# Moving projection work between the query/key tiles, and modulation products into the attention and the merge, in a two-block transformer kernel

## The reference

```python
mod_x = silu(c) @ ada_w + ada_b                      # 6*1024 columns
sh1, sc1, g1, sh2, sc2, g2 = split(mod_x, 6)
hx = modulate(rmsnorm(x, norm1_g), sh1, sc1)         # h * (1 + sc) + sh
px = hx @ w_in                                       # 512 + 256 + 128 + 32 + 2048 columns
fx, qlx, kvlx, krx, gx = split_proj(px)              # Fourier input, latents, gates
kx, vx = mla_kv(kvlx, krx, ...)                      # also for the 256 context rows
qx = mla_q(qlx, ...)                                 # 8 heads of 96, RMS norm and rotation
att_x = latent_attention(qx, keys of x and ctx, values)
g = sigmoid(gx + b_gate)                             # gf | ga, 1024 each
y = gf * (fourier_mix(fx) @ w_fourier) + ga * (att_x @ w_mla_o)
x = x + g1 * (y @ w_out)
x = x + g2 * sq_relu_mlp(modulate(rmsnorm(x, norm2_g), sh2, sc2), w_up, w_down)
```

## Time and profile before

| what | value |
|---|---|
| median of 3 runs | 2515.11 us (2514.92 to 2517.38) |
| the profiled execution: time, span | 2515.88 us, 2514.1 us |
| PE, PEld busy | 93%, 75% of the span |
| DVE, ACT, POOL busy | 40%, 32%, 33% |
| mean granted clock of PE | 0.965 |
| query/key tiles, first sum to first score | 118.13 to 209.55 us |
| attention, first score to last value | 209.55 to 332.6 us |
| Fourier input, then DFT begins | 336.13 to 358.00 us |
| first `wfa` product, last `out1` product | 393.95 and 547.5 us |

### The profile page before, as it was taken

How to read it: one execution, slowest core, us unless ns; L and a number is a source line. 1 busy time by engine, 2 the same in 40 slices (tenths; PEclk the granted TensorE clock), 3 DMA queues, 4 the chain that set the end, 5 groups by cost and what they waited for, 6 DMA issues and landing times.

```text
span 2514.1 us, 29045 instructions
## 1 busy us (share of the span) xinstructions
PE 2329.7 (93%) x11804; PEld 1874.0 (75%) x11804; DVE 998.1 (40%) x1609; ACT 811.5 (32%) x1184; POOL 818.3 (33%) x234
## 2 busy tenths in 40 slices
PE   7758999989999979989898999999899899999998
PEld 3535788867888868878787788667588788788887
DVE  3685623142111246564636320533536345322202
ACT  3333532223222325242424222333423343222212
POOL 0746323433344423020211133122133332344342
PEclk9877999989999989999999999999999899999999
DMA  6412122222332222010101023112123231223321
GB/s 233 134 50 84 51 78 84 93 92 67 101 100 89 95 88 75 26 51 18 51 18 51 17 84 109 51 43 88 46 77 108 79 123 64 81 90 100 100 98 53
DMA packets 178610, 197.47 MB, mean 79 GB/s; under 512 B 3412, under 2 KB 170816, under 8 KB 178496
## 3 DMA queue, kind: packets, MB, share of 16 engines
q1 hardware_dynamic: 176848, 190.84, 23.6%
q10 hardware_dynamic: 1648, 5.02, 0.5%
HBM read 193.76 MB, written 2.10 MB: 78 GB/s over the span
## 4 chain that ended last, share of the span: by engine, by line
PE 81%; DVE 6%; issue 2%; ACT 2%; POOL 1%; DMA 0%; ACTq 0%; DVEq 0%; POOLq 0%
PE ps L1824 20%; PE ps L1826 19%; PE ps L1825 19%; PE ps L2120 3%; PE ps L1924 3%; PE ps L2086 2%; PE ps L2324 1%; PE ps L2315 1%; PE ps L2082 1%; PE ps L2322 1%; POOL w_lo L599 1%; PE ps L1918 1%; PE ps L1871 1%; PE ps L1873 1%; PE ps L1872 1%
## 5 line engine op out<-in xcount | busy, mean ns | idle before, releaser
L599 POOL TENSOR_TENSOR w_lo<-raw,w_hi 128x2048 fp32r<-128x2048 f32 (+1 forms) x150 | 681.1, 4541 | 1485.9 <-ACT w_hi L673 1485.9
L1824 PE MATMUL ps<-h_hi,w_hi 128*128 128x512 f32 x1384 | 561.4, 406 | 21.6 <-POOL w_lo L599 6.0
L1826 PE MATMUL ps<-h_hi,w_lo 128*128 128x512 f32 x1384 | 544.9, 394 | 0.0
L1825 PE MATMUL ps<-h_lo,w_hi 128*128 128x512 f32 x1384 | 544.1, 393 | 0.0
L673 ACT ACTIVATE w_hi<-raw 128x2048 fp32r<-128x2048 f32 x150 | 285.6, 1904 | 395.7 <-PE ps L1826 394.6
L1824 PEld LDWEIGHTS ps<-h_hi,w_hi 128*128 128x128 f32 x1384 | 263.3, 190 | 101.5 <-issue 39.2
L1826 PEld LDWEIGHTS ps<-h_hi,w_lo 128*128 128x128 f32 x1384 | 262.7, 190 | 57.4
L1825 PEld LDWEIGHTS ps<-h_lo,w_hi 128*128 128x128 f32 x1384 | 263.7, 191 | 50.1
L1824 PE MATMUL ps<-g_hi,w_hi 128*128 128x512 f32 x256 | 100.9, 394 | 0.0
L1826 PE MATMUL ps<-g_hi,w_lo 128*128 128x512 f32 x256 | 100.4, 392 | 0.0
L1825 PE MATMUL ps<-g_lo,w_hi 128*128 128x512 f32 x256 | 99.4, 388 | 0.0
(11 more groups left out here) (370 smaller groups left out, 4052.1 us busy)
## 6 DMA issues: line engine op xcount, KB each, us to landing
raw<-w_in SPq DMA_DIRECT2D x48, 1024.0 KB, 5.2
raw<-w_down SPq DMA_DIRECT2D x27, 1024.0 KB, 5.1
raw<-ada_w SPq DMA_DIRECT2D x24, 1024.0 KB, 5.2
raw<-w_gate_up SPq DMA_DIRECT2D x22, 1024.0 KB, 5.1
raw<-w_up SPq DMA_DIRECT2D x16, 1024.0 KB, 5.5
raw<-w_mkv SPq DMA_DIRECT2D x8, 1024.0 KB, 5.6
raw<-w_out SPq DMA_DIRECT2D x4, 1024.0 KB, 5.2
raw<-w_a_out SPq DMA_DIRECT2D x4, 1024.0 KB, 5.2
```

The costliest lines, as they stand in the source:

```text
L599: nc.gpsimd.tensor_tensor(w_lo[:, split_at[u] % 2, 0:n], raw[:, u % 2, 0:n], w_hi[:, split_at[u] % 2, 0:n].bitcast(F32), ALU.subtract).the ...
L1824: T.matmul(out_, wh, hi, start=start, stop=False, skip_group_check=True)
L1825: T.matmul(out_, wh, lo, start=False, stop=False, skip_group_check=True)
L1826: return T.matmul(out_, wl, hi, start=False, stop=stop, skip_group_check=True)
```

## The change

What it does, part by part:

- **Unit order.** `f0` stands before `lat_kv`, `f1` and the four `gf` units behind it; then 12 instead of 16 modulation blocks; the last four stand between the units of the merge.
- **Tiles.** PE does `f0` before `lat_kv`, `f1` in pieces around the latent statistics, and in each of the tiles m = 0 to 7 four pieces of a `gf` unit (`FILL`). ACT stores `gf` as sigmoid at m = 1, 3, 5, 7. The tile's own banks move from 0 and 1 to 2 and 3 for odd m.
- **Residual.** The sigmoid of `gf` is kept in `xT`. `xT` itself is written to DRAM before (2 MB, issued by ACT) and read back in 8 parts during the merge.
- **Modulation.** Eight of the 16 later blocks stay on POOL, which begins them only after the tenth `qk_mm`. Eight go to DVE, with eight chained instructions of 256 columns each: blocks 2, 5, 8 and 11 behind items 11, 17, 23 and 29 of the attention, blocks 12 to 15 at the end of the merge steps j = 0 to 3. The matmuls of `modulation` stand at item 27, behind the attention, and in the MLP.
- **Fourier part.** The DFT begins right behind the attention, with pieces of `ga0` and `ga1` between its steps.

```diff
+    wide("f0", "f", t["w_in"], 0, 0)
     wide("lat_kv", "kv", t["w_in"], 0, FOUR_W + Q_LORA, 4)
-    for j in range(8, 24):
+    wide("f1", "f", t["w_in"], 0, 256)
+    for j in range(4):
+        wide("gf", "gf", t["w_in"], 0, GATE1_COL + 256 * j)
+    for j in range(8, 20):
         wide("ada_b", "ada", t["ada_w"], 0, 256 * j, 0, False)
-    for j in range(2):
-        wide("f", "f", t["w_in"], 0, 256 * j)
-    for j in range(4):
-        wide("merge1", "gf", t["w_in"], 0, GATE1_COL + 256 * j)
-        wide("merge1", "ga", t["w_in"], 0, GATE1_COL + D + 256 * j)
+    MERGE1 = [("ga", 0), ("ga", 1), ("wfa", 0), ("ada", 12), ("ga", 2), ("wfa", 1), ("ada", 13), ("ga", 3), ("wfa", 2),
+              ("ada", 14), ("wfa", 3), ("ada", 15)]
...
+    BY_VECTOR = [2, 5, 8, 11, 12, 13, 14, 15]
+    BY_POOL = [a for a in range(16) if a not in BY_VECTOR]
+    BATCH = [range(0, 8), range(8, 12), range(12, 16)]
+
+    def ada_row_of(a):
+
+        if 8 <= a < 12:
+            return tmp2[:, :, :].rearrange("p a (b c) -> p (a b) c", c=256)[:, a - 8, :]
+        return ada_sum[:, a % 8, :]
...
+    ADA_TURN, ADA_ITEM, ADA_BANK = {11: 2, 17: 5, 23: 8, 29: 11}, 27, [6, 6, 5]
...
+        return 4 if m % 2 == 0 else 2
+
+    FILL = [4] * 8 + [0, 0]
...
+                elif ada_units.index(u - 2) - 8 in BY_POOL:
+                    sp.wait_ge(sem["ada_by_pool"], BY_POOL.index(ada_units.index(u - 2) - 8) + 1)
                 else:
-                    sp.wait_ge(sem["ada_summed"], ada_units.index(u - 2) - 7)
+                    sp.wait_ge(sem["ada_by_vector"], BY_VECTOR.index(ada_units.index(u - 2) - 8) + 1)
...
-            for u in range(first["merge1"]):
+            for u in range(first["merge1"] + 2):
                 load(u)
             sp.wait_ge(sem["at_out"], 32)
             sp.dma_start(dft[:, :], t["dft"]).then_inc(sem["dft_in"], 16)
-            load_phase("merge1")
+            for u in range(first["merge1"] + 2, last_of["merge1"]):
+                load(u)
...
+                if a == 0:
+                    pool.wait_ge(sem["c_silu"], 2)
+                    pool.wait_ge(sem["qk_mm"], 10)
...
+            act.dma_start(x_kept, xT[:, :, :].rearrange("p k c -> p (k c)")).then_inc(sem["x_out"], 16)
...
+                if m in fill_done:
+                    j = fill_done[m]
+                    for jj in range(2):
+                        store_tile(first["gf"] + j, jj, xT[:, 2 * j + jj, :], ACT.Sigmoid, bias=col("b_gate", 2 * j + jj))
+                    if j < 2:
+                        next_hi()
...
-            attention("one", prob1, probT1, QK1 ** -0.5, at_hi, (20, 25))
-
-
-            for j in range(2):
-                for jj in range(2):
-                    store_tile(first["f"] + j, jj, f_T[:, 2 * j + jj, :])
-                next_hi()
+            attention("one", prob1, probT1, QK1 ** -0.5, at_hi, (30, 31))
...
+                        act.dma_start(xT[:, k, :], x_kept[:, k * S:(k + 1) * S]).then_inc(sem["x_back"], 16)
...
+            def modulate(a):
+
+                u, dst = ada_units[8 + a], ada_row_of(a)
+                dve.wait_ge(w_in_slot[u % 2], load_count[u])
+                dve.wait_ge(sem["c_silu"], 2)
+                link(V.tensor_scalar(dst, raw[:, u % 2, 0:256], silu_c[:, 0, 0:1], None, ALU.mult))
+                for k in range(1, KT):
+                    ins = V.scalar_tensor_tensor(dst, raw[:, u % 2, k * 256:(k + 1) * 256], silu_c[:, k, 0:1], dst,
+                                                 ALU.mult, ALU.add)
+                    if k < KT - 1:
+                        link(ins)
+                ins.then_inc(sem["ada_by_vector"], 1)
...
+                    if kind == "one" and n in ADA_TURN:
+                        modulate(ADA_TURN[n])
+                    if kind == "one" and n == ADA_ITEM:
+                        modulation(0)
...
+                modulate(12 + j)
...
+            wide_gemm(first["f0"], h_hi, h_lo)
...
+            for k in range(3, 6):
+                piece(first["f1"], k)
             qk_mm(0)
             qk_mm(1)
+            for k in range(6, KT):
+                piece(first["f1"], k)
+            filled = 0
             for m in range(10):
                 if m < 8:
                     qk_mm(m + 2)
+                for i in range(FILL[m]):
+                    piece(first["gf"] + filled // KT, filled % KT)
+                    filled += 1
                 qk_turn(m)
...
-                wide_gemm(first["f"] + j, h_hi, h_lo)
...
+            for i in range(2):
+                u = merged("ga", i)
+                over_channels(2 * i)
+                over_channels(2 * i + 1)
+                for k in range(5):
+                    piece(u, k)
+                over_tokens(2 * i)
+                over_tokens(2 * i + 1)
+                for k in range(5, KT):
+                    piece(u, k)
+            pe.wait_ge(sem["fm_lo_done"], 4)
...
```

More of the change, by code:

```diff
@@ L414, in tile_count @@
         return val([x + j + 1 for x in tile_at], u, loop)
+    tile_bank, tile_turn = [], []
+    per_bank, n_rot = [0] * 4, 0
+    for u, x in enumerate(units):
+        banks = []
+        for j in range(x.tiles):
+            if first["f1"] <= u < first["ada_b"]:
+                banks.append(j)
+            else:
+                banks.append(n_rot % 4)
+                n_rot += 1
+        tile_bank.append(banks)
+        for b in banks:
+            per_bank[b] += 1
+        tile_turn.append([per_bank[b] for b in banks])
     def bank_of(u, j):
-        return (tile_at[u] + j) % 4
+        return tile_bank[u][j]
     def bank(u, j):
@@ L423, in stored_count, with merged @@
     def stored_count(u, j, loop=None):
-        return val([(x + j) // 4 + 1 for x in tile_at], u, loop)
+        return val([x[j] if j < len(x) else 0 for x in tile_turn], u, loop)
+    def merged(kind, j):
+        return first["merge1"] + MERGE1.index((kind, j))
     def slot_before(u):
@@ L490, in qk_bank @@
     def qk_bank(m):
-        return 4 if m % 2 == 0 else 0
+        return 4 if m % 2 == 0 else 2
+    FILL = [4] * 8 + [0, 0]
+    fill_done, _n = {}, 0
+    for _m, _k in enumerate(FILL):
+        for _i in range(_k):
+            _n += 1
+            if _n % KT == 0:
+                fill_done[_m] = _n // KT - 1
     qk_sq = sq2[:, :, :].rearrange("p a c -> p (a c)")[:, 0:H1 * QK1]
@@ L625, in _ @@
                 if u == first["ada_b"]:
-                    for a in range(16):
+                    for a in BY_POOL:
                         modulate(a)
-                    u += 16
+                    u += 12
                     continue
@@ L766, in _ @@
                 store_tile(u, j, lat_q[:, j, :])
+            next_hi()
+            for j in range(2):
+                store_tile(first["f0"], j, f_T[:, j, :])
+            next_hi()
             store_tile(v, 0, lat_kv[:, 0:S])
@@ L817, in _ @@
             v_and_square(0)
+            for j in range(2):
+                store_tile(first["f1"], j, f_T[:, 2 + j, :])
+            next_hi()
+            act.wait_ge(sem["x_out"], 16)
             for m in range(10):
@@ L1532, in mlp_chunk @@
                                         ALU.subtract).then_inc(sem["g_lo_done"], 1)
+                if isinstance(count0, int) and count0 == 0:
+                    modulation(2)
+                    dve.wait_ge(sem["ada_mod"], 11)
                 for j in range(4):
@@ L1997, in _ @@
                  late=ctx_there)
+            for k in range(3):
+                piece(first["f1"], k)
             pe.wait_ge(sem["lat_sq"], 3)
@@ L2137, in attention @@
                     turned(n)
+                    if kind == "one" and n == ADA_ITEM:
+                        modulation(0)
                 values(b - 1)
-            pe.wait_ge(sem["ada_mod"], 9)
             pe.wait_ge(sem["qk_stored"], 10)
+            stored([first["gf"] + 3])
             attention("one")
```

145 lines of the change are left out of this document (69 added, 76 removed).

## The result

| | before | changed |
|---|---|---|
| median of 4 runs each, on one chip | 2515.02 us (2512.09 to 2517.38) | 2545.57 us (2544.44 to 2547.34) |
| profiled execution: time, span, mean granted clock | as in the table of the kernel before | 2547.34 us, 2545.4 us, 0.958 |

The ratio is 1.0116, with a 95% interval of 1.0103 to 1.013: the change makes the kernel 1.2% slower, some 30 us. The forecast was 2532 with a range from 2508 to 2546. The sign held, and the range only just, by 0.4 us; the narrower range of the forecast itself, 2522 to 2543, did not. The working gave +16.5 us and the profiled execution has +31.5, so about half of the loss was foreseen.

A forecast was written before the change was run, and what follows sets the result against it. PE, busy 93% of the span, was taken as the bound. Terms 10.5 + 12.8 + 21.0 - 21.3 - 8.4 + 1.9 = +16.5 on the profiled 2515.9, less 0.8, gave 2532 us, range 2508 to 2546.

The forecast's parts named there:

- up to the first tile sum: Before the tiles: `f0` and six pieces of `f1` move in, partly covering waits; first sum from 118.1 to 128.6, +10.5 us.
- tiles, to the first score: Ten query/key tiles: gate pieces added, POOL beside tiles 8 and 9; first score at 232.8 instead of 209.55, +12.8 us.
- attention: First score to attention's end: DVE blocks 5 and 8 held behind POOL, block 11 free, `modulation(0)` 3.7; +21.0 us.
- attention to DFT: Between attention and DFT: two `f` units and the old modulation gone, the DFT matrices' load partly uncovered; -21.3 us.
- DFT, to `wfa0`: Fourier part: products and two units between them as before, butterflies covered by pieces and DFT products; 0 us.
- merge and `out1`, norm: Merge: four units gone (-43.6), waits for weights (30.4) and half-speed products (4.8) added; -8.4 us.
- MLP's modulation: In the MLP: a half-size `modulation` added; +1.9 us.
- Rival B: Merge waits are mostly covered, so the slot chain costs half: 2532 - 17.6 = 2514 us; chance 0.08.
- Rival A: Blocks 5 and 8, tiles 8 and 9: DVE's short instructions pass between POOL's, hardly blocked; 2506 us; chance 0.13.
- the eight tiles end at 208: Step in the tiles: from PE at 128.2, with waits of 2.4, 1.5 and 2.5, the first eight end at 208 us.
- C: Tiles: each table switch has a drain, so each return to the root is 1.4 us later; 2537 us; chance 0.05.
- rival D: Loads issued in pairs share the rate, the first landing near 8.3 instead of 5.2; merge and collisions; 2545 us; chance 0.12.

The follow-up runs named there:

- e1: Changed kernel with DVE working modulation blocks 12 to 15 at the start of each merge step, not its end: 2511.16 us, 0.9977 of the kernel before.
- e3: Changed kernel with POOL starting its modulation blocks only when the last tile is normalised, not at the tenth `qk_mm`: 2538.37 us, 1.0086 of the kernel before.
- e2: Changed kernel with modulation blocks 0 to 11 all on POOL, none on DVE in the attention: 2536.71 us, 1.008 of the kernel before.
- e5: Changed kernel with DVE's attention blocks 2, 5, 8, 11 each cut into four parts behind four items: 2540.75 us, 1.0082 of the kernel before.
- e8: e6 with the 32 gate pieces spread over all ten tiles instead of the first eight: 2470.29 us, 0.9804 of the kernel before.
- e6: Changed kernel with the edits of e1, e2 and e3 together: 2479.49 us, 0.984 of the kernel before.
- e10: e8 measured again, unchanged, in more rounds: 2470.98 us, 0.9808 of the kernel before.

## Why the prediction was right, and where its sizes were off

The mechanisms held in the places that the prediction named, but their prices were 14 to 15 us too low, and that the range from 2508 to 2546 still held the result, by 0.4 us, is luck. Term by term, from the positions of the same events before and after:

| term | predicted | measured |
|---|---|---|
| up to the first tile sum | +10.5 | +8.9 |
| tiles, to the first score | +12.8 | +19.0 |
| attention | +21.0 | +25.8 |
| attention to DFT | -21.3 | -21.3 |
| DFT, to `wfa0` | 0 | +1.7 |
| merge and `out1`, norm | -8.4 | -6.1 |
| MLP's modulation | +1.9 | +1.8 |
| the rest | 0 | +1.5 |
| sum | +16.5 | +31.3 of the span |

**Right: the merge.** Waits of 7.9, 7.9, 10.7 and 3.9 were predicted, 30.4 in all; measured 7.44, 7.92, 10.46 and 4.42, 30.2 in all. e1 shows the cause, since nothing but the place of the block was moved. Rival B (half covered) is out.

**Right: POOL's lock.** In tiles 8 and 9, 9 and 11 were predicted and 9.23 and 11.62 came; e3 took 12.7 us of waits away, tile 7's included. Two of DVE's four attention blocks were held up, as forecast, by blocks 6 and 9 of POOL, for PE waits of 7.9 and 5.4; e2 brought back 20.8 us in the attention. Rival A (short instructions pass between POOL's) is out. The Trainium skill ("SBUF — State Buffer", Who interferes with whom) states it as a lock that the later of the two waits for: a DVE instruction with two SBUF inputs waits out a POOL instruction that reads SBUF; one with a single input doesn't, unless it runs in one of the two-port modes, which `tensor_scalar` can enter; the reduction never does. The trace agrees in the cases seen: in a tile beside POOL the reduction over SBUF took 0.94 us, as it did when free, the products of two SBUF operands took up to 4.25 instead of 0.96, and the scaling, a `tensor_scalar`, up to 4.07 instead of 0.62 (e5).

**Right: attention to DFT.** 21.3 came back, and the DFT waits 2.2 us for its matrices, behind a modulation of 1.95 that covers the rest of the load.

**Mis-sized: the tiles, by 6.2 us.** The step "the eight tiles end at 208" failed: they ended at 211.6, though the first sum came 1.6 earlier than forecast, and tiles 8 and 9 took 1.0 more than the 24.8 put. The waits in them were 3.25, 2.47 and 3.18 where 2.4, 1.5 and 2.5 had been put (2.5 together). And I had given PE's work behind them its full-clock length: the four products behind the first two waits took 3.37 and 3.40 instead of 1.88, 3.0 more, and the transposes of tile 7 took 1.94 instead of 1.08. In the merge I had costed slow products behind three of the four waits; behind the short waits of the tiles I had put them at nothing.

**Mis-sized: the attention, by 4.8 us.** The two blocked blocks were put at 15.5. They cost 18.4 by the distance of ACT's copies from their period of 3.55: 8.6 and 6.1 in the waits and the slow transposes right behind them, and 2.5 and 1.2 in the items behind, whose products ran at half clock (0.50 in the 3.5 us behind the first). The modulation was put at its own 3.7 and cost 5.2, for the products behind it ran slowly too:

```profile
362.05 3.63 PE L2156 MATMUL ps<-const,ada_sum 128*128 128x1 f32 x32
...
367.59 2.56 PE L2217 MATMUL ps<-probT,v 128*64 128x128 f32 x12
```

2.56 where 1.52 is usual. Another 1.3 us stand behind the free block 11. PE had waited 0.90, 1.22 and again 0.90 us in turn, and the next values ran at half clock:

```profile
379.93 2.78 PE L2217 MATMUL ps<-probT,v 128*64 128x128 f32 x12 [0.90 <-ACT probT L912]
```

The copy of a weight unit on ACT at that point, which the prediction had left out, held nobody up: it ended at 381.7, and ACT then waited for PE until 383.9. In e3, with the same three waits, these values took 1.52, so this share too differs between executions.

**Mis-sized: DFT and merge, 4 us together.** The first DFT step took 5.29 us at the lower clock instead of 3.62. The merge's 2.3 us more are mostly slow products: by the starts of the products against 0.227 us at full clock, 2.1, 1.5, 1.5 and 1.5 us were lost behind the four waits, 6.6 in all where 4.8 had been put, for the fourth wait had been given none. The waits are right to 0.2 us, and some 0.6 stays undivided. The last 1.5 us, behind the MLP's modulation, stay open too: PE's waits from 600 us on have the same names and nearly the same lengths as before.

**Rivals C and D.** C, a drain behind each table load, is out. ACT of the changed kernel in tile 1:

```profile
153.32 1.28 ACT L879 ACT_TABLE_LOAD   x1
154.62 0.30 ACT L879 ACTIVATE qk_stat<-qk_stat,one_eps 128x8 f32<-128x8 f32 x1
```

The store before the load ends at 153.31, and the root starts 0.02 us behind the load, so there is no drain on either side. So 2545 was reached, but not by the way of C, nor of D (loads in pairs): issued at 446.05 with the block's load right behind, the unit was there at 451.04, 5.0 us later. First in, first out fits that.

So the nearness of rival D's 2545 to the result is chance. What the forecast lacked, 14 to 15 us, has mostly one source, work of PE at half clock that it had not priced: 3.9 us in the tiles, 3.7 behind the blocked blocks, 1.5 behind the modulation, 1.3 behind block 11, 1.7 in the DFT and 1.8 in the merge. The waits of the tiles were 2.5 us longer than put, and the terms that came out smaller make up for part of it.

**Where the expected gain went.** 65.4 us of units stand ahead of the first score in place of later, and the waits of the tiles, which part of them fills, were 44.2 long before. The pieces earn it: in e8 the first score is only 8.6 us later than before, with the 65.4 done (the old stretch also held the modulation of 6.83 in the earlier trace rows). In the changed kernel the gain was lost again in three places by the new place of the modulation work: 35 us in the merge (e1), some 14 in tiles 7 to 9 (e3), 21 in the attention (e2), 69 together (e6).

## What to carry to other kernels

A small job that is moved to "idle" time on another engine also holds its buffer: ask when the buffer must be free for the next load, and put the job ahead of the engine's waiting work, not behind it. Here one call put ahead of eight instructions, not behind them, was worth 35 us. When two engines lock each other out, hold the one off that has time, wherever the other is on the critical path, and look where it runs next: an edit in one place (e2) can lengthen the lock in another. And price a wait of PE at more than its length: behind each of the four waits of 4.4 to 10.5 us in the merge, half-speed products cost 1.5 to 2.1 us more. Behind waits of 2.5 to 3.3 us it was as much or more in some executions and nothing in others.

## What the runs showed of the hardware

**The granted clock can fall at short waits already.** In the changed kernel PE was idle for 3.25 us before tile 0 and for 2.47 before tile 2. In the 2 us before it started again for tile 0 the granted clock was still 1.00, in the 5 us behind it 0.66 (window columns as in the earlier trace rows):

```profile
138.00:140.00 2.00, 0.10 (x1) 0.10 (x2) 1.90 (x6) 0.00 (x0) 0.00 (x0) 1.00 0.93 293
140.00:145.00 5.00, 5.00 (x16) 2.84 (x17) 3.62 (x7) 3.96 (x6) 0.00 (x0) 0.66 0.23 81
```

The drop comes late here, when PE is at work again, so it costs more than the wait alone suggests. It need not come: behind a wait of 2.53 us in e5 (PE starts at 347.80) the clock stayed at 1.00, and behind the same 3.25 us in e10 too.

**When it falls differs between executions of one kernel.** e8 and e10 are the same kernel, run on two chips, with the same waits of 3.25 and 2.45 to 2.46 us, and have different slow rows: the transposes behind the first wait took 1.94 us in e8 and 1.08 in e10, and from tile 0 to tile 1 it was 10.84 and 8.11 us. That is 2.7 us between two executions with identical work, and one reason why differences under 5 us could not be told apart here.

**Behind products of one column the clock fell in some executions and not in others.** In the changed kernel it was 0.56 for 3 us behind the 32 products of 128x1, though PE had been busy without a gap:

```profile
362.00:366.00 4.00, 4.00 (x35) 3.81 (x34) 0.25 (x3) 1.69 (x3) 0.00 (x0) 1.00 0.79 227
366.00:369.00 3.00, 3.00 (x11) 1.94 (x10) 1.84 (x5) 0.00 (x0) 0.00 (x0) 0.56 0.14 47
```

In e3, which does the same there, it stayed at full speed behind them:

```profile
355.00:358.00 3.00, 3.00 (x19) 2.04 (x18) 2.12 (x7) 0.00 (x0) 0.00 (x0) 1.00 0.03 8
```

It stayed at 1.00 in the kernel before too, in the 3 us behind the 32 products that end at 336.1, and behind the 28 products of one column at 115 to 118 us of the changed kernel. So these products are not enough to slow down what follows them, and what decides it stays open.
